# GpSimd's clear of the even FoX queries set behind the next remainders, and one weight load behind the gathers of the rope rows, in a two-layer hybrid decoder kernel

## What is computed

```
a = rms_norm(h, attn_norm); proj = a @ w_in            # 15 column groups
dq, dk, iq, ik: (rms_norm and) partial rope on 16 of 64 columns of a head
o_a = dsa_attention(...)      # index scores choose the top 128 keys, then softmax
fq, fk = rms_norm per head;  o_b = forgetting_attention(fq, fk, fv, log_f)
o_c = gla_chunked(...)        # gated linear attention
h = h + concat(o_a, o_b, o_c) @ w_out
h = h + (silu(f @ w_gate) * (f @ w_up)) @ w_down,  f = rms_norm(h)
```

## Time and profile before

| | us |
|---|---|
| median of 3 runs | 1249.98 (1249.91 to 1250.82) |
| the profiled execution | 1250.16 |
| its span, first to last instruction | 1248.4 |
| PE busy in it | 1234.3 (99%) |
| DVE busy | 1026.9 (82%) |
| ACT busy | 699.2 (56%) |
| POOL busy | 172.5 (14%) |

### The profile page before, as it was taken

How to read it: one execution, slowest core, us unless ns; L and a number is a source line. 1 busy time by engine, 2 the same in 40 slices (tenths; PEclk the granted TensorE clock), 3 DMA queues, 4 the chain that set the end, 5 groups by cost and what they waited for, 6 DMA issues and landing times.

```text
span 1248.4 us, 23731 instructions
## 1 busy us (share of the span) xinstructions
PE 1234.3 (99%) x9344; PEld 1182.2 (95%) x9344; DVE 1026.9 (82%) x1692; ACT 699.2 (56%) x1158; POOL 172.5 (14%) x120
## 2 busy tenths in 40 slices
PE   7999999999999999999999999999999999999999
PEld 7999999999999999999998989888899999998998
DVE  5777789588999999897665898885889999989865
ACT  6666547656555555753354774486665555558332
POOL 2564213100000000000024462131000000000000
PEclk9999999999999999999999999999999999999999
DMA  5322111132332221233323222110322332212333
GB/s 199 97 73 86 52 35 35 35 135 71 133 102 102 102 102 69 85 102 116 105 86 100 92 70 67 34 52 18 135 102 102 124 113 102 102 69 85 118 119 119
DMA packets 27131, 113.74 MB, mean 91 GB/s; under 512 B 3344, under 2 KB 3984, under 8 KB 21648
## 3 DMA queue, kind: packets, MB, share of 16 engines
q1 hardware_dynamic: 26304, 111.18, 26.4%
q10 hardware_dynamic: 720, 1.09, 0.2%
HBM read 108.79 MB, written 2.10 MB: 89 GB/s over the span
## 4 chain that ended last, share of the span: by engine, by line
PE 94%; DVE 2%; POOL 2%; issue 1%; ACT 1%; DMA 1%; SPq 0%; POOLq 0%; DVEq 0%; ACTq 0%
PE ps L1387 22%; PE ps L1393 11%; PE ps L1002 11%; PE ps L1104 6%; PE ps L1098 6%; PE ps L1099 6%; PE ps L1008 5%; PE ps L1471 5%; PE ps L1507 4%; PE ps L1228 3%; PE ps L1476 2%; PE ps L1512 2%; PE ps L1176 2%; PE ps L1201 1%; PE ps L1211 1%
## 5 line engine op out<-in xcount | busy, mean ns | idle before, releaser
L1098 PE MATMUL ps<-xhi,whi 128*128 128x264 f32 (+1 forms) x616 | 174.3, 311 | 0.0
L1099 PE MATMUL ps<-xlo,whi 128*128 128x264 f32 (+1 forms) x616 | 167.5, 300 | 0.0
L882 POOL TENSOR_TENSOR wlo<-raw,whi 128x1024 fp32r<-128x1024 f32 x48 | 118.6, 2474 | 179.1 <-ACT whi L1685 178.5
L1098 PEld LDWEIGHTS ps<-xhi,whi 128*128 128x128 f32 x616 | 116.1, 188 | 4.8 <-issue 0.8
L1099 PEld LDWEIGHTS ps<-xlo,whi 128*128 128x128 f32 x616 | 116.2, 189 | 3.5
L1685 ACT ACTIVATE whi<-raw 128x1024 fp32r<-128x1024 f32 x74 | 77.9, 1054 | 49.8 <-PE ps L1008 30.4
L1104 PE MATMUL ps<-xhi,wlo 128*128 128x264 f32 (+1 forms) x616 | 100.5, 305 | 0.5 <-POOL wlo L882 0.5
L1104 PEld LDWEIGHTS ps<-xhi,wlo 128*128 128x128 f32 x616 | 85.2, 188 | 5.0 <-POOL wlo L882 0.7
L1387 PE MATMUL ps<-fhi,hi_a 128*128 128x264 f32 (+1 forms) x352 | 88.2, 283 | 0.0
L1387 PE MATMUL ps<-flo,hi_a 128*128 128x264 f32 (+1 forms) x352 | 88.1, 282 | 0.0
L1387 PE MATMUL ps<-flo,hi_b 128*128 128x264 f32 (+1 forms) x320 | 80.3, 283 | 0.0
(11 more groups left out here) (373 smaller groups left out, 3857.0 us busy)
## 6 DMA issues: line engine op xcount, KB each, us to landing
raw<-in_weights SPq DMA_DIRECT2D x116, 512.0 KB, 3.5
raw<-in_groups SPq DMA_DIRECT2D x42, 1024.0 KB, 4.8
out_hT<-h SPq DMA_DIRECT2D x7, 256.0 KB, 4.5
h<-in_hT SPq DMA_DIRECT2D x4, 264.0 KB, 6.4
h<-in_hT ACTq DMA_DIRECT2D x4, 264.0 KB, 5.8
cst<-in_consts SPq DMA_DIRECT2D x1, 780.5 KB, 9.1
xnb<-feat SPq DMA_DIRECT2D x10, 66.5 KB, 2.1
feat<-xnb SPq DMA_DIRECT2D x10, 66.5 KB, 2.1
```

The lines of the kernel that those rows point to most:

```text
L882: nc.gpsimd.tensor_tensor(wlo[:, b], raw[:, b], whi[:, b].bitcast(F32), ALU.subtract).then_inc(split_done, 1)
L1098: nc.tensor.matmul(o, whi[:, k % 2, n], xhi[:, n, cut], start=(n == 0), stop=False)
L1099: nc.tensor.matmul(o, whi[:, k % 2, n], xlo[:, n, cut], start=False, stop=False)
```

## The change

Three strings of steps are edited, and one wait is added.

- First layer, POOL: `clear_even` and `square_parts(8)` change places. It was: remainder of u11, clear_even, square 8, remainder of u12. It is: remainder of u11, square 8, clear_even, remainder of u12.
- Second layer, POOL: it was spread_sums, clear_even, remainder of u12, square 9, remainder of u13. It is spread_sums, remainder of u12, square 9, clear_even, remainder of u13.
- Second layer, SP: it was gather(0), load of u4, load of u5, gather(1), gather(2), load of u6. It is gather(0), load of u4, gather(1), gather(2), load of u5, load of u6.
- `clear_even` waits, before it writes, until POOL's own squares issued so far are done.

```
-     POOLE: "AAQAQAAACACAQAAQCACAAQAAAQAAAACACCCAAA",
+     POOLE: "AAQAQAAACACAQAACQACAAQAAAQAAAACACCCAAA",
...
-     POOLE: "QAAQAAAAACACCAAQQACAQAAAAAQAAACACCAAAC",
-     DMAE: "EAAEEAGAAEEAGAAAAAAAAAAAAAAAAAA"},
+     POOLE: "QAAQAAAAACACCAAQACQAQAAAAAQAAACACCAAAC",
+     DMAE: "EAEEAAGAAEEAGAAAAAAAAAAAAAAAAAA"},
...
-                split, zeroed = [2 + l * UNITS], [0]
+                split, zeroed, halved = [2 + l * UNITS], [0], [0]
...
                 def clear_even():
                     pool.wait_ge(split_done, 2 + split[0])
+                    pool.wait_ge(ev.sq_split, halved[0])
                     pool.wait_ge(ev.parted, 2)
...
                     nc.gpsimd.tensor_tensor(sq_parts[:, 0], sqb[:, 0], sq_parts[:, 1].bitcast(F32), ALU.subtract).then_inc(ev.sq_split, 1)
+                    halved[0] += 1
```

## The result

The changed kernel takes 1252.60 us, the one before 1250.16 in the runs beside it: a ratio of 1.0018, 95% interval 1.0012 to 1.0025. That is 2.4 us more, outside the range of 1248.3 to 1252.3, and it goes the slower way where next to no change was forecast. It is still within the 0.2% (2.5 us) that the forecast counts as no change, but the interval lies clear of 1. The rival "step 6 is lost" had said +2.1.

A forecast was written before the change was run, and what follows sets the result against it. PE was taken to bound the kernel, busy 1234.3 of 1248.4 us. The terms -0.61 - 1.01 + 1.58 = -0.04 on a profiled 1250.16, with the median 0.18 lower, gave 1249.9 us, range 1248.3 to 1252.3.

The forecast's parts named there:

- step 6 is lost: Rival: second layer, u13's subtraction on POOL starts before DVE's third index sum; +2.1 us in all, 1252.1; chance 0.28.
- First layer, POOL, -0.61: Square 8 ends well ahead of norm(8), so PE's hole before norm(8) goes: -0.61 us, bounds 0 to 0.7 gained.
- Second layer, SP, -1.01: gather(2) lands earlier with u5's load behind it, so PE's hole before the rope's product goes: -1.01 us, bounds 0 and -1.1.
- PE's 0.5 us wait for u12 saves nothing, gate(0) decides: Second layer: removing PE's 0.5 us wait for u12's remainder gains nothing, as gate(0) waits for ACT about 10 us later.
- the bound of -0.7: Second layer, POOL: best case of that term, with no meeting of DVE's sums and POOL's subtractions at all, -0.7 us.
- DVE's sums and POOL's subtractions take turns: Second layer: of DVE's two-SBUF-operand sum and POOL's subtraction, whichever starts first finishes first; a held-up sum took 2.00 against 0.64 us.
- steps 1 to 5: Second layer: u12 and square 9 delay DVE's first two sums, the second 2.94 us late; u13's subtraction would start near 726.50.
- Step 6: Second layer: DVE's third index sum, 0.03 us ahead of u13's subtraction, takes 0.64 us and ends 1.58 late.
- +1.58: Second layer, POOL term: DVE's third sum, and with it the relu, ACT's run and gate(0), come 1.58 us late.
- the prediction's bound (3.71 - 1.58): Second layer, POOL: +3.71 us is the upper bound, if u13's subtraction precedes the third sum; +1.58 is the forecast term.
- 0.41: Chance given to the forecast itself, 1249.9 us, in which DVE's third sum goes ahead of u13's subtraction.

The follow-up runs named there:

- e5: Changed kernel with second-layer POOL doing u13's remainder before clear_even and holding u12's remainder until DVE's first two index sums are done; 1247.85 us, ratio 0.9980.
- e4: Changed kernel with u13's remainder ahead of clear_even in the second layer's POOL order, no wait added; 1250.65 us, ratio 1.0001.
- e7: Changed kernel with clear_even's one memset written as four, each over a quarter of the same columns; 1250.58 us, ratio 1.0002.
- e2: Kernel before with only the second layer's POOL order changed (with its wait), first layer and load as before; 1254.10 us, ratio 1.0032.
- e3: Changed kernel with second-layer POOL holding u13's remainder until DVE's third index sum is done; 1250.70 us, ratio 1.0003.

## Why the prediction was wrong

- *First layer, POOL, -0.61*: right. -0.57 to -0.63 in every profile that has the edit.
- *Second layer, SP, -1.01*: right, -1.0 to -1.1, and by its own mechanism: gather(2) lands 2.0 us after its issue instead of 3.8, and u5 is rounded when PE frees its slot.
- *PE's 0.5 us wait for u12 saves nothing, gate(0) decides*: right. The wait is gone and gate(0) waits longer. e5 shows the other half: once DVE is not late, PE's wait is worth having. With -1.01, e5 even passes the bound of -0.7. That bound is the idle time of PE's two waits as the profile counts it (0.5 + 0.2); the other two holes, measured from start to start, were wider than their idle time, too (0.61 against 0.45, and 1.01 against 0.84).
- *DVE's sums and POOL's subtractions take turns; steps 1 to 5*: right, to about 0.1 us. The first two sums took 2.65 and 1.56 against 2.61 and 1.64 by my steps. On the page "SBUF — State Buffer", section "SBUF: two separate sides", the Trainium skill has the lock that this looks like, with the condition that a VectorE instruction with two SBUF inputs meets it only against a GpSimd instruction that reads SBUF. The traces agree: the sum that ran inside the memset, which reads nothing, took its 0.64, the memset that began during a sum its 0.99 (e4), and the sum that met a copy 0.85 (e7).
- *Step 6, the third sum is ahead by 0.03 us and so wins*: wrong, and this alone makes the forecast wrong. I took the order of recorded starts as deciding. The sum was recorded 0.05 ahead in the changed kernel and 0.04 in e2, and lost both times; so for this sum a lead of 0.05 us is not enough. The sum took 2.88 instead of 0.64, and +1.58 became +3.92. Of this the lost race is 2.16 by the runs (3.92 against 1.76 in e4, which has the same first two sums), 2.13 by the prediction's bound (3.71 - 1.58), and the other 0.2 is a sum of small errors: DVE, which moved up by 2.04 us against PE's 2.16, began its first sum 0.12 later in PE's terms than I had it.
- *The rival was there, the weights were not*: "step 6 is lost" had the mechanism, the place and +2.1 us. With a lead of 0.03 us against gaps that I myself put at 0.04 to 0.1, its 0.28 beside 0.41 was too little, and a range that ended at 1252.3 left the rival's own 1252.1 only 0.2 us for the errors of the steps before it. Of the 0.30 by which the time passes the range, 0.18 is the kernel before itself: 1249.98 was the median of 3 runs, that of 17 is 1250.16.

What was not foreseen, and did not decide: PE's largest new wait is not at gate(0) but 15 us before, at the turn of the meta tokens' probabilities (line 1238, 1.9 us), as ACT's exponentials stand in its order behind the relu that waits for the first sum. These waits are no losses that could be taken away one by one: as ACT sets the time of gate(0), PE would reach it earlier without the first two and wait longer there.

## What to carry to other kernels

When a step is moved on a little-used engine, ask not only whom its own results make late but which resource it holds while it runs: swapping a memset (harmless to VectorE here) with two subtractions made VectorE 3.9 us late although GpSimd was no busier. Where VectorE and GpSimd instructions would start within 0.1 us of each other, either price both orders as equally likely or fix the order by a wait; a wait on the little-used engine, with an order to fit it (e5), took the second layer's part here from +3.92 to -1.01 us. And a hole in TensorE's work is worth its length only if the next step that waits is not waiting for somebody else.

## What the runs showed of the hardware

For the index sum, a recorded lead of 0.05 us (changed kernel) and 0.04 (e2) over a GpSimd subtraction was not enough: GpSimd went first. That is no rule for VectorE at large. Other VectorE instructions with two SBUF operands went first with leads about as small: one of 0.01 over a subtraction in the kernel before, and one of 0.06 in e2 (DVE, then POOL, in that order):

```profile
790.79 0.43 DVE L2467 TENSOR_TENSOR state<-state,coef 128x256 f32<-128x256 f32 x1
790.80 2.66 POOL L882 TENSOR_TENSOR wlo<-raw,whi 128x1024 fp32r<-128x1024 f32 x1 [8.73 <-ACT whi L1685]
...
61.76 0.70 DVE L2261 TENSOR_TENSOR xnb<-xnb 64x532 f32<-64x532 f32 x1
61.81 1.85 POOL L967 TENSOR_TENSOR sq_parts<-sqb,sq_parts 128x532 fp32r<-128x532 f32 x1 [9.36 <-ACT sq_parts L1758]
```

Here the DVE instructions keep their usual times, and POOL's take 2.66 instead of 2.40 and 1.85 instead of 1.33. So two recorded starts this close don't tell which goes first. Why the sum loses is not shown. An estimate points at the instruction: a sum that is held up ends 0.43 after the subtraction, while alone it takes 0.64, so it would get its turn some 0.2 us after its recorded start, and a VectorE instruction that needs less time to its turn would win with a smaller lead.

An instruction held up in this way is recorded as starting when it was issued, not when it got its turn, so its duration holds the wait: 2.88 instead of 0.64 in the changed kernel.

One profile, that of e3, had a second surprise. PE had been idle for 1.86 us, ahead of the same product as in the changed kernel, and then its granted clock fell to half, 1.2 of 2.4 GHz, for about 3.4 us; the columns are as in the page's windows (length, busy time and count by engine, granted clock, DMA share, GB/s):

```profile
715.00:723.00 8.00, 6.33 (x42) 5.54 (x40) 7.70 (x13) 4.64 (x11) 6.76 (x6) 1.00 0.07 9
723.40:726.60 3.20, 3.20 (x9) 2.52 (x9) 2.99 (x9) 3.10 (x6) 2.26 (x4) 0.50 0.30 122
726.80:730.00 3.20, 3.20 (x21) 2.84 (x20) 3.00 (x11) 0.77 (x2) 2.00 (x1) 1.00 0.09 18
```

In that stretch matmuls of 512 columns start every 0.43 us (724.18, 724.61), behind it every 0.23 (730.31, 730.54). In the table e3 is 0.8 us later than e4 at gate(0), and I put that down to the slower stretch. The rows of ACT and PE at gate(0) of e3 fit this:

```profile
735.91 0.39 ACT L1803 ACTIVATE v_fox<-ps 128x256 f32<-128x256 f32 x1
...
736.87 0.51 PE L1168 MATMUL ps<-lr_parts,w_parts 80*128 80x266 f32 x2
```

ACT is done at 736.30, and PE comes 0.57 later and without a wait; in e4 it waits there for ACT (0.51). This cause was not tested by itself. The profiles of the changed kernel, e2, e4 and e7 have the same idle time of 1.8 to 1.9 us at that product and show no such fall. So a wait of PE may cost more than its length, and in some executions only. In the timed runs the mean granted clock is below 1.000 in two of the 11 of e3 (0.998 and 0.999, its two slowest, 1251.68 and 1251.57) and in one of the 7 of e2 (0.999, its slowest, 1255.57), and in no other of any kernel here.
